# Streamed weights of a hybrid decoder layer, copied once to DRAM piece by piece

## Chip, core, metric

One core of a Trainium2 chip runs one launch of the kernel. The metric is the device time of the launch in microseconds, the median over the runs shown.

## What is computed

One layer of a hybrid decoder, for 1024 prompt tokens, 16 meta tokens and 64 sample tokens (8 sequences of 8), model width 1024, all in float32. The steps, cut to what matters:

```python
hn = rmsnorm(x, norm_mix_w);  proj = hn @ w_in              # u, z, xbc, dt
g = gelu(s5(u));  y_s5 = rmsnorm(g * sigmoid(g @ w_glu))     # w_glu 1024 x 1024
y_m2 = mamba2(z, xbc, dt)                                    # conv, scan by chunks of 128, gate, norm
x = x + concat([y_s5, y_m2]) @ w_out                         # w_out 2048 x 1024
h = rmsnorm(x, norm_ffn_w)
q = h @ w_q                                                  # w_q 1024 x 2048: 8 heads x 2 halves
idx, gate = top16_of_sums(q @ sub_keys)                      # product keys, 128 experts per token
y = rmsnorm(x + sum_k gate_k * gelu(u_tab[idx_k] . h) * v_tab[idx_k])
```

## The kernel before

The program runs in stages, with a barrier of all engines between them: projection (`project_tokens`), S5 scan (`s5_scan`), Mamba (`mamba_scan`), and a last stage, `route_and_experts`, that does mixing, routing and experts. Tokens are handled in 9 tiles of 128 rows: 8 of the prompt and one of the samples and meta tokens. Weights and constants are laid out on the host (`lay_out`): `w_glu`, `w_out` and `w_q` lie in DRAM as 128 partitions x 8 (or 16) row blocks x columns.

**Mamba.** The second half of `mamba_scan` goes over the 8 prompt tiles. On the queue of the sync engine (SP) `load(i)` brings the tile's window for the convolution (`m2s_window`, L1119) and its time steps (`m2s_dt_raw`, L1120), and `store(i)` writes the tile's result `y` to `scratch_ym` (L1124). SP issues `load(0)`, then for each i waits for `window_free`, issues `load(i + 1)` and `store(i)`. VectorE handles tile k in this order: tokens and their product with dt, the first three taps of the convolution of tile k + 1 (`first_taps`, which waits for both transfers of `load(k)`), the decays of tile k, the last tap of tile k + 1, the state and the output of tile k. There is one window buffer. TensorE, ScalarE and GpSimd work on the same tile between VectorE's steps.

**The last stage.** Its tiles are mixed and routed in blocks of 1, 2, 3 and 3 tiles (`BLOCK_OF`). The first block, the opening, runs alone. Then a loop goes over all 1088 row sets of the experts (`NT`): for each, GpSimd gathers 128 expert rows of 8 KB into one of 7 ring buffers (L1521), VectorE takes a dot product (L1812), ScalarE makes the weights (L1621, L1623), and TensorE adds the weighted rows to an accumulator (L1831), after which the ring buffer is free. The steps of block 1 are written into the program between the row sets of tile 0, those of block 2 between the row sets of block 1, those of block 3 between those of block 2; each engine runs its list in order. The last weight load is issued at 3547 us; after the steps of block 3 only row sets remain.

Every block streams all of `w_glu`, `w_out` and `w_q` again, as 20 pieces of 1 MB (128 partitions x 8 row blocks x 256 columns): 4 for `pe_glu` (L1854), 8 for `pe_o` (L1879), 8 for `pe_q` (L1893). Two buffers, `w_buf[:, W % 2]`, take turns: SP's step `sp_w` (`weights`, L1444 to L1461) waits until TensorE is done with the piece two before, then issues the load, and TensorE waits for `w_in` ahead of the piece's first matmul. In SBUF a piece is 8 KB in a row for each partition; in DRAM it is 8 separate runs of 256 floats, 1 KB each:

```python
rows = D["w_q"][:, :, (s - QUERY) * COLS:(s - QUERY + 1) * COLS]
sp.dma_start(w_buf[:, W % WB], rows).then_inc(w_in[W % WB], 16)
```

Of the kernel before, what the change touches and what calls it, by code (L numbers as in the profile page):

```python
# [5 lines left out]
F32 = mybir.dt.float32  # L6
# [6 lines left out]
P = 128  # L13
D_MODEL = 1024
KT = D_MODEL // P
# [36 lines left out]
PH = 8  # L52
# [3 lines left out]
EXPERTS = NK * NK  # L56

LAG = Q + 1
TWO_PI = 2.0 * np.pi
PI_HI = 6.28125  # L60
PI_LO = float(np.float32(TWO_PI - PI_HI))
ROUND = 1.5 * 2.0 ** 23
# [25 lines left out]
def s5_tables(nc, ctx):  # L88

    sb = lambda n, s: ctx.enter_context(nc.sbuf_tensor("s5_" + n, s, F32))  # L90
    return {"power": sb("power", [P, 2, PAIRS, LAG]),
            "down": sb("down", [P, 2, PAIRS, Q]),
# [18 lines left out]
def project_tokens(nc, D, tables):  # L111


    with ExitStack() as ctx:
# [67 lines left out]
        def _(pool):  # L182
# [7 lines left out]

            chain.link(nc.gpsimd.tensor_scalar(T(8), T(2), 1.0 / TWO_PI, ROUND, ALU.mult, ALU.add))
            chain.link(nc.gpsimd.tensor_scalar(T(8), T(8), ROUND, None, ALU.subtract))
# [27 lines left out]

            for n in range(2, LAG):
                complex_mult(power[:, 0, :, n], power[:, 1, :, n], power[:, 0, :, n - 1],
# [168 lines left out]
def s5_scan(nc, D, tables):  # L391
# [4 lines left out]
    with ExitStack() as ctx:  # L396
# [3 lines left out]
        ident = sb("ident", [P, P])  # L400
        out_w = sb("out_w", [P, PAIRS, 2, LAG * S5_CH])
        in_w = sb("in_w", [P, PAIRS, 2, Q * S5_CH])
# [5 lines left out]
        with ExitStack() as c2:  # L408
            sb2 = cur(c2)
            c_in = sb2("c_in", [P, 2, PAIRS, S5_CH])  # L410
            skip = sb2("skip", [S5_CH, S5_GROUPS])
            prod = sb2("prod", [P, PAIRS // 2, LAG, S5_CH])
            prod2 = sb2("prod2", [P, PAIRS // 2, LAG, S5_CH])
            skip_eye = sb2("skip_eye", [S5_CH, S5_GROUPS, S5_CH])
# [48 lines left out]
            def _(dve):  # L463
# [18 lines left out]
                def output_weights(pairs):  # L482

                    shape = [P, PAIRS // 2, LAG, S5_CH]
                    lagged = lambda h: power[:, h, pairs].unsqueeze(3).to_broadcast(shape)
# [308 lines left out]
                        last.then_inc(r_made, 1)  # L794


def mamba_scan(nc, D):


# [2 lines left out]
    with ExitStack() as ctx:  # L802
        sb = lambda n, s, d=F32: ctx.enter_context(nc.sbuf_tensor("m2s_" + n, s, d))
        sem = ctx.enter_context(stage_semaphores(nc, "m2_"))
# [305 lines left out]

        with ExitStack() as c2:
            conv_tail = c2.enter_context(nc.sbuf_tensor("m2m_conv_tail", [P, XB, TAPS - 1], F32))
            prompt_out, tail_ready, window_free = sem("prompt_out"), sem("tail_ready"), sem("window_free")
            block = c2.enter_context(nc.Block())

            @block.sync
            def _(sp):
                def load(i):
                    sp.dma_start(window[:], D["xbc"][:, :, bass.ds(i * P + N_META - TAPS + 1, P + TAPS - 1)]).then_inc(tile_in, 16)  # L1119
                    sp.dma_start(dt_raw[:], D["dt"][bass.ds(i * P, P), :]).then_inc(tile_in, 16)  # L1120

                def store(i):
                    sp.wait_ge(y_ready, i + 3)
                    sp.dma_start(D["ym"][bass.ds(i * P, P), :], y[:].rearrange("p h d -> p (h d)")).then_inc(y_out, 16)  # L1124

                load(0)
                with sp.Fori(0, MAIN_TILES - 1) as i:
                    sp.wait_ge(window_free, i + 1)
                    load(i + 1)
                    store(i)  # L1130
                store(MAIN_TILES - 1)
                sp.wait_ge(state_ready, MAIN_TILES + 2)
                sp.dma_start(D["ssm_end_prompt"], state[:]).then_inc(prompt_out, 16)
                sp.wait_ge(tail_ready, 1)
                sp.dma_start(D["conv_end_prompt"], conv_tail[:]).then_inc(prompt_out, 16)
                sp.wait_ge(prompt_out, 32)
                sp.wait_ge(y_out, 16 * (MAIN_TILES + 2))
# [110 lines left out]
def route_and_experts(nc, D):  # L1248
# [10 lines left out]
    RING = 7  # L1259
    WB = 2  # L1260
    GROUPS, PER = 4, 32
    COLS = D_MODEL // GROUPS
    BLOCK_OF = ((0,), (1, 2), (3, 4, 5), (6, 7, 8))
    NB = max(len(tiles) for tiles in BLOCK_OF)
    FIRST = [tiles[0] for tiles in BLOCK_OF]
# [1 line left out]
    NT = MAIN_TILES * SLOTS + SAMPLE  # L1267
    NG = NT // PER
    UNITS, UNIT = 4, 4
    PIECES = 4 + 8 + PH  # L1270
    GLU, OUT, QUERY = 0, 4, 12

    def block_steps(nb):

# [48 lines left out]
    for b, tiles in enumerate(BLOCK_OF):  # L1323
# [4 lines left out]
        s, room = FIRST[b - 1] * SLOTS, len(BLOCK_OF[b - 1]) * SLOTS - 26  # L1328
# [16 lines left out]
    with ExitStack() as ctx:  # L1345
        sb = lambda n, s, d=F32: ctx.enter_context(nc.sbuf_tensor("pe_" + n, s, d))
        sem = ctx.enter_context(stage_semaphores(nc, "pe_"))
# [6 lines left out]
        ffn_w = sb("ffn_w", [P, D_MODEL])  # L1354
        final_w = sb("final_w", [P, COLS])
        norm_w = sb("norm_w", [P, 2 * KT])
# [3 lines left out]
        w_buf = sb("w_buf", [P, WB, KT, COLS])  # L1360
# [48 lines left out]
        w_in = [sem(f"w_in{n}") for n in range(WB)]  # L1409
# [25 lines left out]
        @block.sync  # L1435
        def _(sp):
            for t, n in ((ident, "ident"), (ones, "ones"), (fold_ident, "fold_ident"), (norm_w, "mix_norm_w"), (ffn_w, "norm_ffn_w"),
                         (count16, "count16"), (keys_t, "keys_t")):
                sp.dma_start(t[:], D[n]).then_inc(consts_in, 16)
            for j in range(GROUPS):  # L1440
                rows, cols = slice(j * PER, j * PER + PER), slice(j * COLS, j * COLS + COLS)
                sp.dma_start(final_w[rows, :], D["final_norm_w"][rows, cols]).then_inc(consts_in, 16)

            def weights(b, s):  # L1444
                W = PIECES * b + s
                if W >= WB:
                    b0, s0 = divmod(W - WB, PIECES)
                    if s0 < OUT:
                        sp.wait_ge(glu_made, KT * b0 + 2 * s0 + 2)
                    elif s0 < QUERY:  # L1450
                        sp.wait_ge(out_made, outs(b0, (s0 - OUT) // 2, s0 % 2, size(b0) - 1))
                    else:
                        sp.wait_ge(q_made, PAIR * b0 + 2 * (s0 - QUERY) + 2)
                if s < OUT:
                    rows = D["w_glu"][:, :, s * COLS:(s + 1) * COLS]
                elif s < QUERY:
                    q, half = divmod(s - OUT, 2)
                    rows = D["w_out"][:, KT - KT * half:2 * KT - KT * half, q * COLS:(q + 1) * COLS]
                else:
                    rows = D["w_q"][:, :, (s - QUERY) * COLS:(s - QUERY + 1) * COLS]  # L1460
                sp.dma_start(w_buf[:, W % WB], rows).then_inc(w_in[W % WB], 16)  # L1461

            def step(name, args):
                if name == "sp_w":
                    weights(*args)
                if name == "sp_y":
                    b, i = args
                    k = FIRST[b] + i
                    if k:
                        pb, pi = HOME[k - 1], k - 1 - FIRST[HOME[k - 1]]  # L1470
                        sp.wait_ge(turned, TURN["pe_m", (pb, pi)] + 1)
                        sp.wait_ge(h_root, FIRST[b])
                        if i == 0:
                            sp.wait_ge(turned, TURN["pe_h", (pb, pi)] + 1)
                    for t, n in ((y5, "y5"), (z, "z"), (ym, "ym")):
                        sp.dma_start(t[:], D[n][k * P:k * P + P, :]).then_inc(y_in, 16)
                if name == "sp_x0":
                    b, i = args
                    k = FIRST[b] + i
                    if b:  # L1480
                        sp.wait_ge(x_mid_out, 16 * FIRST[b])
                        sp.wait_ge(h_ready, FIRST[b])
                    sp.dma_start(x_mid[:, i, :], D["x_all"][k * P:k * P + P, :]).then_inc(x_in, 16)
                if name == "sp_xm":
                    b, i = args
                    k = FIRST[b] + i
                    sp.wait_ge(out_taken, kept(b, 3, i))
                    sp.dma_start(D["x_mid"][k * P:k * P + P, :], x_mid[:, i, :]).then_inc(x_mid_out, 16)
                if name == "sp_x":
                    k = args[0]  # L1490
                    sp.wait_ge(x_mid_out, 16 * (FIRST[HOME[k]] + size(HOME[k])))
                    if k:
                        sp.wait_ge(seeded, GROUPS * k)
                    sp.dma_start(x_now[:], D["x_mid"][k * P:k * P + P, :]).then_inc(x_now_in, 16)
                if name == "sp_st":
                    G = args[0]
                    sp.wait_ge(y_ready, G + 1)
                    for j in range(GROUPS):
                        sp.dma_start(D["y"][G * PER:G * PER + PER, j * COLS:(j + 1) * COLS],
                                     out[j * PER:(j + 1) * PER, G % 2, :]).then_inc(y_out[G % 2], 16)  # L1500

            for name, args in opening:
                step(name, args)
            for n in range(NT):
                for name, args in after[n]:
                    step(name, args)
            for r in range(2):
                sp.wait_ge(y_out[r], 64 * (NG // 2))
# [528 lines left out]
```

## Time and profile before

| | |
|---|---|
| median of 3 runs | 4697.36 us (4696.14 to 4698.72) |
| the profiled execution's own time | 4696.99 us |
| its span, first to last instruction | 4695.2 us |
| TensorE / VectorE / ScalarE / GpSimd busy | 2874.7 / 2492.3 / 1336.4 / 1389.4 us |
| moved by DMA | 1333.53 MB, mean 284 GB/s |
| Mamba's prompt tiles | about 1042 to 1354 us |
| opening (block 0, no gathers) | about 1354 to 1529 us |
| first gather issued | 1529.22 us |

Views are read as follows. A busy time is the sum of an engine's instructions; register, semaphore and DMA-issuing instructions are not counted. The DMA share is the mean busy share of the core's 16 DMA engines; it can come out a little above 1. The DMA queue q0 carries the gathers that GpSimd issues, q1 everything that SP issues.

### The profile page before, as it was taken

The numbers are of one execution on the slowest core, as the hardware profiler recorded it, in microseconds if no ns is written. First come the engines' busy times: TensorE is split into PE (matmuls) and PEld (weight loads), VectorE is DVE, ScalarE is ACT, GpSimd is POOL, SyncE is SP. The second block draws the span as 40 slices with busy tenths as digits, with TensorE's granted clock in tenths as the row PEclk, the third lists the DMA queues.
The fourth block names the chain that finished last, engine by engine and source line by source line (L and its number), as shares of the span: only waits on it lengthen the run. The fifth ranks groups of instructions, "written<-read, shape, count | busy, mean of one in ns | idle before, by whom it ended". The sixth has DMA issues, their size and how long they took to land.

```text
span 4695.2 us, 49395 instructions
## 1 busy us (share of the span) xinstructions
PE 2874.7 (61%) x17200; PEld 1544.7 (33%) x17200; DVE 2492.3 (53%) x5167; ACT 1336.4 (28%) x3229; POOL 1389.4 (30%) x1530
## 2 busy tenths in 40 slices
PE   8999590745555587348876544786666544444444
PEld 5767460723344364114532111353222111111110
DVE  1000529248845339744369955544677864454454
ACT  1110120112221533244333325523333333332322
POOL 3000320301100223333343344333444443333333
PEclk9999755866768798559987655897777555555555
DMA  4111300121135799999999899999999999999999
GB/s 163 55 46 36 75 2 2 43 99 30 46 109 163 287 345 346 348 374 354 365 415 386 339 416 418 409 390 395 414 395 382 403 420 419 420 420 420 420 419 372
DMA packets 337161, 1333.53 MB, mean 284 GB/s; under 512 B 65168, under 2 KB 181776, under 8 KB 197136
## 3 DMA queue, kind: packets, MB, share of 16 engines
q0 software_dynamic: 156672, 1140.92, 59.8%
q1 hardware_dynamic: 180288, 190.03, 12.4%
q8 instruction: 113, 1.85, 0.2%
q14 instruction: 88, 0.72, 0.0%
HBM read 1288.61 MB, written 40.09 MB: 283 GB/s over the span
## 4 chain that ended last, share of the span: by engine, by line
DMA 31%; PE 15%; DVE 15%; ACT 5%; issue 5%; POOL 1%; SPq 0%; DVEq 0%; POOLq 0%; ACTq 0%
DMA pe_ring<-in_uv,pe_index 27%; DVE pe_ring L1812 6%; PE pe_bg L1879 4%; PE pe_acc L1831 4%; DMA pe_w_buf<-in_w_out 3%; PE pe_bg L1854 3%; PE pe_bg L1893 3%; DVE pe_cand L1631 2%; ACT pe_weight L1623 1%; ACT pe_mark L1621 1%; DVE pe_picked L1715 1%; ACT L1621 1%; PE pe_ps_t L1921 1%; DVE pe_best_i L1658 1%; DMA pe_ym<-scratch_ym 1%
## 5 line engine op out<-in xcount | busy, mean ns | idle before, releaser
L1812 DVE CUSTOM_DVE_ANT_0 pe_ring<-pe_ring,pe_h_rep 128x1024 f32<-128x1024 f32 x1088 | 1322.8, 1225 | 1001.3 <-DMA pe_ring<-in_uv,pe_index 978.9
L1521 POOL DMA_INDIRECT pe_ring<-in_uv,pe_index x1088 | 1183.0, 1087 | 2165.6 <-PE pe_acc L1831 1799.7
L1831 PE MATMUL pe_acc<-pe_ring,pe_weight 128*32 128x256 f32 x8704 | 963.7, 537 | 1264.8 <-ACT pe_weight L1623 1241.1
L1831 PEld LDWEIGHTS pe_acc<-pe_ring,pe_weight 128*32 128x32 f32 x8704 | 212.1, 128 | 1955.6 <-ACT pe_weight L1623 1822.4
L1621 ACT ACTIVATE pe_mark<-pe_eye,pe_dot 128x32 f32<-128x32 f32 x1088 | 348.2, 320 | 1629.3 <-DVE pe_dot L1812 1592.6
L1623 ACT ACTIVATE pe_weight<-pe_mark,pe_choice 128x32 f32<-128x32 f32 x1088 | 349.7, 321 | 35.1
L1893 PE MATMUL pe_bg<-pe_in_t,pe_w_buf 128*128 128x384 f32 (+2 forms) x1024 | 322.7, 477 | 9.9 <-DMA pe_w_buf<-in_w_q 8.8
L372 PE MATMUL pj_bank<-pj_w_in,pj_normed_t 128*128 128x512 f32 (+1 forms) x720 | 268.3, 530 | 5.1 <-DMA pj_w_in<-in_w_in 5.1
L1893 PEld LDWEIGHTS pe_bg<-pe_in_t,pe_w_buf 128*128 128x128 f32 x1024 | 205.9, 227 | 130.1 <-issue 67.4
L378 PE MATMUL pj_bank<-pj_normed_t,pj_w_in 128*128 128x128 f32 x1728 | 195.2, 275 | 0.0
L378 PEld LDWEIGHTS pj_bank<-pj_normed_t,pj_w_in 128*128 128x128 f32 x1728 | 193.7, 192 | 0.0
L372 PEld LDWEIGHTS pj_bank<-pj_w_in,pj_normed_t 128*128 128x128 f32 x720 | 126.7, 192 | 141.3 <-issue 141.3
L1879 PE MATMUL pe_bg<-pe_w_buf,pe_m_t 128*128 128x256 f32 x576 | 143.0, 404 | 19.2 <-DMA pe_w_buf<-in_w_out 19.2
L1879 PE MATMUL pe_bg<-pe_w_buf,pe_s_t 128*128 128x256 f32 x576 | 136.8, 392 | 17.2 <-DMA pe_w_buf<-in_w_out 16.1
L1854 PE MATMUL pe_bg<-pe_in_t,pe_w_buf 128*128 128x384 f32 (+2 forms) x512 | 138.6, 427 | 1.6 <-DMA pe_w_buf<-in_w_glu 1.5
L1879 PEld LDWEIGHTS pe_bg<-pe_w_buf,pe_m_t 128*128 128x128 f32 x576 | 113.3, 202 | 50.1 <-DMA pe_w_buf<-in_w_out 22.0
L954 PE MATMUL m2p_a<-m2s_x_dt,m2s_decay 128*128 128x64 f32 x288 | 63.4, 421 | 106.8 <-DVE m2s_decay L850 106.8
L440 POOL MEMSET s5s_b_apart<- 128x512 f32 x1 | 0.5, 524 | 426.2 <-POOLq L108 426.2
L1879 PEld LDWEIGHTS pe_bg<-pe_w_buf,pe_s_t 128*128 128x128 f32 x576 | 109.2, 194 | 45.2 <-DMA pe_w_buf<-in_w_out 18.3
L1621 ACT ACT_TABLE_LOAD x95 | 121.9, 1283 | 5.1 <-DVE pe_dot L1812 3.5
L314 DVE COPY pj_chan_out<-pj_bank 128x512 f32<-128x512 f32 x18 | 12.4, 692 | 192.0 <-PE pj_bank L378 192.0
L1854 PEld LDWEIGHTS pe_bg<-pe_in_t,pe_w_buf 128*128 128x128 f32 x512 | 93.2, 203 | 43.3 <-issue 6.8
(303 smaller groups left out, 3364.7 us busy)
## 6 DMA issues: line engine op xcount, KB each, us to landing
pe_w_buf<-in_w_out SPq DMA_DIRECT2D x32, 1024.0 KB
pe_w_buf<-in_w_q SPq DMA_DIRECT2D x32, 1024.0 KB
pe_ring<-in_uv,pe_index POOLq DMA_INDIRECT x1088
pe_w_buf<-in_w_glu SPq DMA_DIRECT2D x16, 1024.0 KB
m2s_window<-scratch_xbc SPq DMA_DIRECT2D x8, 786.0 KB
pj_w_in<-in_w_in SPq DMA_DIRECT2D x1, 6144.0 KB, 38.8
scratch_xbc<-pj_chan_out SPq DMA_DIRECT2D x8, 768.0 KB, 5.2
pj_x<-in_x_all SPq DMA_DIRECT2D x9, 512.0 KB
```

Of the source, the lines that this page charges most:

```text
L372: last = nc.tensor.matmul(b[:, 0:w], x_t[:, k, :], w_in[:, k, a:a + w], start=k == 0, stop=k == KT - 1)
L378: last = nc.tensor.matmul(b[:, c * P:(c + 1) * P], w_in[:, k, a:a + P], x_t[:, k, :], start=k == 0, stop=k == KT - 1)
L954: last = nc.tensor.matmul(ps_a[:, h // HPG, (h % HPG) * HD:(h % HPG + 1) * HD], decay[:, h, :], x_dt[:, h, :], start=True, stop=True)
L1521: nc.gpsimd.indirect_dma_start(out=ring[:, n % RING, :], out_offset=None, in_=D["uv"], in_offset=bass.IndirectOffsetOnAxis(ap=row, axis=0) ...
L1621: A(mark[:, p, :], eye[:], ACT.Gelu_apprx_tanh, scale=dot[:, p:p + 1]).then_inc(mark_ready, 1)
L1623: A(weight[:, p, :], mark[:, p, :], ACT.Copy, scale=choice[:, k % 2, 1, s:s + 1]).then_inc(weight_ready, 1)
L1631: tt = lambda o, a, b, op: V.tensor_tensor(out=o, in0=a, in1=b, op=op)
L1812: V.tensor_tensor_reduce(out=ring[:, p, 0:D_MODEL], in0=ring[:, p, 0:D_MODEL], in1=h_rep[:, G % 2, :], scale=1.0, scalar=0.0, op0=ALU.mult ...
L1831: last = T.matmul(acc[j * PER:(j + 1) * PER, G % 2, 0:COLS], lhs(j), src[:, j * COLS:(j + 1) * COLS], start=first, stop=final)
L1854: last = T.matmul(bg[:, c % 2, 0:width(b)], w_buf[:, W % WB, kk, c % 2 * P:(c % 2 + 1) * P], wide(in_t_all, b)[:, kk, :], start=kk == 0, s ...
L1879: last = T.matmul(bg[:, (q * size(b) + i) % 4, 0:COLS], src[:, kk, i * P:(i + 1) * P], w_buf[:, W % WB, kk, :], start=half == 0 and kk == ...
L1893: last = T.matmul(bg[:, j % 2, 0:width(b)], w_buf[:, W % WB, kk, j % 2 * P:(j % 2 + 1) * P], wide(in_t_all, b)[:, kk, :], start=kk == 0, s ...
```

## The change

A new DRAM tensor `packed` of 20 pieces, each 128 x 8 x 256 floats in one contiguous block of 1 MB, is written at the start of Mamba's prompt tiles. SP issues the 20 copies, DRAM to DRAM, right after `load(0)`, each with the same source as the weight load that it stands for. At the end of that stage SP waits until all are written. In the last stage `weights` loads `D["packed"][s]` in place of the slice of the weight tensor, for all four blocks, so that a partition's share of a piece is one run of 8 KB. The constants for the pieces move to the top of the file. Nothing else differs.

```diff
+def weight_piece(D, s):
+    if s < OUT:
+        return D["w_glu"][:, :, s * COLS:(s + 1) * COLS]
+    if s < QUERY:
+        q, half = divmod(s - OUT, 2)
+        return D["w_out"][:, KT - KT * half:2 * KT - KT * half, q * COLS:(q + 1) * COLS]
+    return D["w_q"][:, :, (s - QUERY) * COLS:(s - QUERY + 1) * COLS]
...
+            D["packed"] = nc.dram_tensor("scratch_packed", (PIECES, P, KT, COLS), F32).ap()
+            packed_out = sem("packed_out")
...
                 load(0)
+                for s in range(PIECES):
+                    sp.dma_start(D["packed"][s], weight_piece(D, s)).then_inc(packed_out, 16)
                 with sp.Fori(0, MAIN_TILES - 1) as i:
                     sp.wait_ge(window_free, i + 1)
                     load(i + 1)
                     store(i)
                 store(MAIN_TILES - 1)
+                sp.wait_ge(packed_out, 16 * PIECES)
...
-                if s < OUT:
-                    rows = D["w_glu"][:, :, s * COLS:(s + 1) * COLS]
-                elif s < QUERY:
-                    q, half = divmod(s - OUT, 2)
-                    rows = D["w_out"][:, KT - KT * half:2 * KT - KT * half, q * COLS:(q + 1) * COLS]
-                else:
-                    rows = D["w_q"][:, :, (s - QUERY) * COLS:(s - QUERY + 1) * COLS]
-                sp.dma_start(w_buf[:, W % WB], rows).then_inc(w_in[W % WB], 16)
+                sp.dma_start(w_buf[:, W % WB], D["packed"][s]).then_inc(w_in[W % WB], 16)
```

## Rows read from the trace of the kernel before

**Rows 1.** The page's 40 slices of the span: GB/s moved by DMA.

```profile
GB/s 163 55 46 36 75 2 2 43 99 30 46 109 163 287 345 346 348 374 354 365 415 386 339 416 418 409 390 395 414 395 382 403 420 419 420 420 420 420 419 372
```

**Rows 2.** The page's DMA queues (packets, MB, share of 16 engines) and issues.

```profile
q1 hardware_dynamic: 180288, 190.03, 12.4%
...
pe_w_buf<-in_w_out SPq DMA_DIRECT2D x32, 1024.0 KB
...
pe_ring<-in_uv,pe_index POOLq DMA_INDIRECT x1088
```

**Rows 3.** Windows: busy us (count) of PE, PEld, DVE, ACT, POOL; clock, DMA share, GB/s.

```profile
1072.00:1354.00 282.00, 149.13 (x521) 99.90 (x519) 217.90 (x191) 61.03 (x78) 38.55 (x14) 0.69 0.11 34
...
1585.00:1760.00 175.00, 144.14 (x832) 101.13 (x832) 63.95 (x115) 70.02 (x141) 42.57 (x41) 0.94 0.88 315
1760.00:2060.00 300.00, 156.93 (x1028) 75.67 (x1026) 225.66 (x658) 99.80 (x248) 101.21 (x90) 0.67 0.93 362
2105.00:2330.00 225.00, 190.90 (x1104) 118.22 (x1100) 97.43 (x169) 92.81 (x198) 75.81 (x66) 0.93 0.93 351
2330.00:2500.00 170.00, 119.37 (x714) 55.74 (x715) 114.95 (x297) 62.16 (x157) 64.98 (x59) 0.79 1.02 416
...
2905.00:3050.00 145.00, 99.69 (x594) 43.60 (x594) 76.56 (x127) 80.01 (x160) 55.93 (x52) 0.79 1.02 410
3050.00:3205.00 155.00, 124.04 (x794) 88.44 (x794) 69.14 (x121) 39.45 (x112) 51.71 (x46) 0.89 0.98 381
3205.00:3560.00 355.00, 224.27 (x1386) 95.67 (x1378) 232.10 (x587) 123.88 (x323) 149.56 (x132) 0.71 1.01 408
4000.00:4500.00 500.00, 238.96 (x1676) 53.17 (x1676) 251.31 (x413) 152.29 (x432) 191.70 (x198) 0.53 1.01 420
```

**Rows 4.** Chain of waits in order of time: start us, us, what.

```profile
1389.71 5.99 DMA pe_w_buf<-in_w_glu
...
2272.91 16.85 DMA pe_w_buf<-in_w_out
...
3104.65 25.43 DMA pe_w_buf<-in_w_out
```

**Rows 5.** TensorE's waits: opening, blocks 1, 2, 3; us in total, times, longest.

```profile
PE pe_bg L1879 <- DMA pe_w_buf<-in_w_out: 5.2, 5, 2.3
...
PE pe_bg L1893 <- DMA pe_w_buf<-in_w_q: 8.3, 2, 5.8
...
PE pe_bg L1879 <- DMA pe_w_buf<-in_w_out: 3.6, 2, 3.2
...
PE pe_bg L1879 <- DMA pe_w_buf<-in_w_out: 26.6, 3, 11.5
```

**Rows 6.** DMA queues of 1385:1460, 2330:2500, 3050:3205, 4000:4500; packets, MB, share.

```profile
q1 hardware_dynamic: 14651, 15.16, 63.3%
...
q1 hardware_dynamic: 4861, 5.59, 9.4%
...
q1 hardware_dynamic: 7616, 8.00, 14.9%
...
q0 software_dynamic: 28514, 207.68, 100.1%
```

**Rows 7.** Timeline of SP and VectorE, Mamba: start, us, instruction, idle time before.

```profile
1042.73 0.55 SPq L1119 DMA_DIRECT2D m2s_window<-scratch_xbc  x1
1063.53 0.58 SPq L1119 DMA_DIRECT2D m2s_window<-scratch_xbc  x1
...
1048.16 1.76 DVE L850 TENSOR_TENSOR m2s_conv<-m2s_window,m2s_conv_w 128x1536 f32<-128x1536 f32 x1 [16.29 <-DMA m2s_dt_raw<-scratch_dt]
1071.76 1.76 DVE L850 TENSOR_TENSOR m2s_conv<-m2s_window,m2s_conv_w 128x1536 f32<-128x1536 f32 x1 [0.23 <-DVE m2s_x_dt L850]
```

**Rows 8.** DMA issues (median us to landing); the weight line (ns min/median/max).

```profile
scratch_y<-in_x_all SPq DMA_DIRECT2D x1, 192.0 KB, 2.8
...
L1461 SPq DMA_DIRECT2D pe_w_buf<-in_w_q x32: 539/545/550, 1431.7 to 3547.3; - x32
```

More of the change, by code:

```diff
@@ L58 @@
 LAG = Q + 1
+COLS = 256
+PIECES, GLU, OUT, QUERY = 20, 0, 4, 12
 TWO_PI = 2.0 * np.pi
@@ L1261, in route_and_experts @@
     GROUPS, PER = 4, 32
-    COLS = D_MODEL // GROUPS
+    assert COLS == D_MODEL // GROUPS and PIECES == 4 + 8 + PH
     BLOCK_OF = ((0,), (1, 2), (3, 4, 5), (6, 7, 8))
@@ L1269, in route_and_experts @@
     UNITS, UNIT = 4, 4
-    PIECES = 4 + 8 + PH
-    GLU, OUT, QUERY = 0, 4, 12
     def block_steps(nb):
```

## Prediction

> **What bounds the kernel now.** The page's slices came first, for the shape [rows 1]: in the first two fifths of the span the 16 DMA engines are nearly idle, from the middle on they move 340 to 420 GB/s. There the expert rows arrive (1088 gathers of 128 rows of 8 KB), and beside them the streamed weights in 1-KB runs, 80 pieces of 1 MB: 32 of w_out as shown [rows 2], 32 of w_q and 16 of w_glu alike. The stage windows [rows 3] then say what limits each stretch; I read TensorE's and VectorE's busy time against the length and the DMA share. 4000 to 4500 has no weights: DMA 1.01, 420 GB/s, everything else half idle. 1585 to 1760 and 2105 to 2330 are TensorE's (144.1 of 175, 190.9 of 225). 1760 to 2060 is VectorE's (225.7 of 300). 2330 to 2500 and 2905 to 3560 are DMA's (0.98 to 1.02), though 3050 to 3205 reaches only 381 GB/s. The opening, up to 1530, has no gathers yet: a serial chain of weight loads and matmuls. The Mamba stage, 1072 to 1354, is VectorE's: 217.9 of 282.
>
> Third came the chain of waits and TensorE's wait list, for what the weights cost today. Nine weight loads stand among the chain's long pieces, of which one for each stretch is shown [rows 4]: four of up to 6 us in the opening, two of up to 17 in block 2, three of some 25 in block 3. The loads are long because the two DMA queues share the engines: a piece is 64 runs per engine, and 25.43 us / 64 = 0.40 us per run, about one 8-KB gather run (8192 B at 420/16 GB/s is 0.31 us) plus one 1-KB run (2.89 us per MB, below, is 0.047 us). So the engines appear to alternate run by run. But much of each load is covered by other matmuls: TensorE stood still for weights only 5.2 us in the opening, 8.3 in block 1, 3.6 in block 2 and 26.6 in block 3 (the largest entry of each) [rows 5].
>
> **What a run costs.** From the DMA views [rows 6], share times window over MB: weights in 1-KB runs alone (1385 to 1460) 0.633 x 75 / 15.16 = 3.13 us per MB of all 16 engines; beside gathers (3050 to 3205) 0.149 x 155 / 8.00 = 2.89; gathers in 8-KB runs (4000 to 4500) 1.001 x 500 / 207.68 = 2.41. A piece is 1.049 MB: 3.28 or 3.03 us now, 2.53 us in 8-KB runs, a saving of 0.75 us where nothing else runs and 0.50 us beside gathers.
>
> **Added: the copies.** Twenty pieces, 20.97 MB, each read in 1-KB runs. They are issued right behind load(0), and load(1) stands behind all of them in SP's program. All of SP's transfers are one queue, q1 [rows 2]. load(0) is issued at 1042.73 and VectorE starts on it at 1048.16, 5.4 us later; load(1) is issued at 1063.53 and its first use is at 1071.76, with 0.23 us of idle time, so it is in time today [rows 7]. SP issues a 1-MB transfer in about 0.5 us [rows 8], 11 us for twenty, so the engines and not SP set the pace. If the queue is served in order, the copies stream from about 1047.5, and at the uncontended 3.13 us per MB take 65.7 us, to 1113.2. load(1) then needs at most its 5.4 us: 1118.6, and 4 us if its start-up hides under the copies. First use goes from 1071.8 to about 1118: **46 us lost**. Nothing covers it: the first taps of tile 2 stand ahead of the decays and the output of tile 1 in VectorE's order, so VectorE idles, and TensorE, ScalarE, GpSimd and SP's store(0) behind it. The later loads come 35 us apart with the copies gone, and the stage's end moves by the whole amount. The new wait for the copies at the stage's end costs nothing: they are done 230 us earlier.
>
> Bounds of this: no transfer of this size from DRAM to DRAM is in the trace. The nearest row is a 192-KB one, landed in 2.8 us [rows 8], no worse than the stores around it. Below: 2.89 us per MB gives 60.6 us and a loss of 41; if the copies kept the 8-KB pace of 2.41, 50.5 us and 31. Above: if reads and writes together can't pass the 420 GB/s that is the most any row shows, 41.9 MB take 100 us and the loss is 80. I take 46, as read runs of this shape were measured at that pace.
>
> **Changed: 80 loads in 8-KB runs.** By stretch:
> - Opening: four loads are on the chain [rows 4], 0.75 us each: 3.0 us. Bounds 0 and the 5.2 us that TensorE waits.
> - Block 1: 8.3 us of waits on two w_q pieces, in the stretch that is VectorE's; a piece beside gathers will land in 8 x (0.31 + 0.31) = 5 us, so the waits go, but VectorE's work remains. I take 5, between 0 and 8.3. No DMA saving is counted while its share is 0.88 to 0.93.
> - Block 2: the 3.6 us wait stands in TensorE's stretch and goes whole. In 2330 to 2500, 5.59 MB fall from 0.094 x 170 = 16.0 to 13.5 us, 2.5 us. Together 6; bounds 2.5 and 3.6 + 20 x 0.50 = 13.6.
> - Block 3, 3050 to 3205: three waits of together 26.6 us, during which the ring of seven rows fills and gathers stop. TensorE's busy time is 124.0, so without the waits DMA is next: the 381 GB/s x 155 us = 59.1 MB at 420 GB/s are 140.6 us instead of 155, **14.4 us**. This holds both the freed stalls and the shorter runs. Bounds 8 (a wait half removed) and 26.6.
> - Block 3, the other 12 pieces, with DMA at 1.01: 12 x 0.50 = 6; I take 5, as 3400 to 3560 is partly VectorE's; bounds 3 and 10.
>
> Sum of gains 3 + 5 + 6 + 14.4 + 5 = 33.4 us; bounds 13.5 and 63.7. The issue on SP stays one instruction per piece. Net: 46 - 33.4 = +12.6 us. The profiled execution took 4696.99 us by its own time, 1.8 more than its span, and the median is 4697.36; on the median, 4710 us.
>
> **A rule against the change.** Shorter runs are dearer here: 2.89 to 3.13 against 2.41 us per MB [rows 6]. The Trainium skill, page "DMA: Bandwidth & Descriptors", section "Specifications", puts the least transfer for line rate at 512 B; by that a 1-KB run would already be at full rate, and the rows of this case differ. As a mechanism it is the third rival below.
>
> **The rivals.**
> 1. *The weights were worth more (faster).* All of TensorE's waits for weights become time (5.2 + 8.3 + 3.6 + 26.6 = 43.7) and block 2 and 3's forty pieces save 0.50 us each (20): 63.7 us; with the copy at its lower 41 us the time is 4675. For it: the 25-us loads on the chain. Against: DMA at 0.98 to 1.02 leaves no room for more than 14 us in 3050 to 3205. It decides once the gain passes 55 us. Chance 0.12.
> 2. *The copies are bound by DRAM, reading and writing at once.* 100 us, loss 80, net +47: 4744. For it: no row shows such a stream. Against: the 2.8-us row. Chance 0.15. The Trainium skill, page "HBM Reference", section "Specifications (TRN2)", gives 716 GB/s for the memory of two cores, an estimate of 58.6 us for 41.9 MB by itself, no bound here; no run here shows it.
> 3. *The run's length buys nothing in rate.* The gains lose opening 3, block 2's 2.5, block 3's 5 and 8.00 MB x 0.48 = 3.8 us: 19 remain, net +27: 4724. Against it stand [rows 6]. Chance 0.05.
> 4. *load(1) isn't held behind the copies*, or they hide: loss under 15 us, net -20: 4677. For it: the DMA engines are at 0.11 in that stage. Against: one queue, one order of issue. Chance 0.08.
> 5. *The loads still come in 1-KB runs.* Only the 46 us remain: 4743. Against: the copy is laid out as the buffer is. Chance 0.03.
>
> **Numbers.** The forecast case, a stall of 41 to 52 us against gains of 28 to 42, holds 0.57 and runs from -1 to +24, that is 4696 to 4721. A measurement of this kernel tells a change from none at about 0.2%, 9.4 us. Of the 0.57, 0.35 lies above +9.4 and 0.22 within it. Slower: 0.35 + 0.15 + 0.05 + 0.03 = 0.58. Faster: 0.12 + 0.08, less 0.05 for weak forms that stay within 9.4 us: 0.15. Same: 0.22 + 0.05 = 0.27. The range goes to 4685 below, leaving out the stronger half of rivals 1 and 4, and to 4742 above, leaving out the worse half of rival 2.
>
> **What would show it.** Right: VectorE idle some 46 us before its first convolution of tile 2, released by tile 2's loads; SP issuing 20 copies in 1044 to about 1100; q1 packets down from 180288 by 81920 - 10240 - 20480, if a copy counts 1-KB runs; TensorE's waits for weights under 10 us in all; 3050 to 3205's work, moved, at 410 GB/s or more; no weight load over 10 us on the chain. Wrong: a stall under 30 or over 60 us; waits for weights that stay; or these waits gone and the gathers' stretch no shorter, which would mean that DMA was the bound there all along.

## The result

The changed kernel takes 4718.41 us, median of 6 runs (4716.02 to 4722.68), against 4697.81 us for the kernel before (6 runs): a ratio of 1.0043, 95% interval 1.003 to 1.0056. It is slower by about 20 us. The prediction said 4710 us and slower, with a range of 4685 to 4742.

The loss comes in one place. In the timeline of SP and of VectorE (start us, us, instruction, idle time before it and what ended it), the kernel after shows, as the counterpart of [rows 7] (the first three copies one by one, the others merged by tensor):

```profile
1045.05 0.60 SPq L1142 DMA_DIRECT2D scratch_packed<-in_w_glu  x1
1045.69 1.55 SPq L1142 DMA_DIRECT2D scratch_packed<-in_w_glu  x1
1047.28 2.73 SPq L1142 DMA_DIRECT2D scratch_packed<-in_w_glu  x1
...
1052.73 27.21 SPq L1142 DMA_DIRECT2D scratch_packed<-in_w_out  x8
1079.98 29.27 SPq L1142 DMA_DIRECT2D scratch_packed<-in_w_q  x8
1109.62 3.15 SPq L1133 DMA_DIRECT2D m2s_window<-scratch_xbc  x1
...
1121.02 1.76 DVE L862 TENSOR_TENSOR m2s_conv<-m2s_window,m2s_conv_w 128x1536 f32<-128x1536 f32 x1 [48.66 <-DMA m2s_dt_raw<-scratch_dt]
```

Before, load(1) was issued at 1063.53 and VectorE used it with 0.23 us of idle time. Now SP gets to it at 1109.62, since it is held at the copies: the first goes out in 0.60 us, the second in 1.55, the third in 2.73, and the last sixteen take about 3.5 us each, which is the pace at which the engines move them (below). VectorE then idles 48.66 us. The DMA queue of 1048 to 1113 (packets, MB, share of 16 engines) gives the pace:

```profile
DMA packets 20038, 20.10 MB, mean 309 GB/s; under 512 B 400, under 2 KB 20038, under 8 KB 20038
...
q1 hardware_dynamic: 20038, 20.10, 101.7%
```

1.017 x 65 / 20.10 = 3.29 us per MB, 69.0 us for the 20.97 MB, or 3.45 us for one copy. The last stage's first transfer goes from 1354.00 to 1400.67: 46.7 us lost by the end of the Mamba stage, of which 1.0 us was there before its load(0) (1042.73 to 1043.71).

The gain comes in the last stage. TensorE's waits for weights (line, cause: us in total, times, longest), from 1340 to 1600 and from 1600 to 2020, as the counterpart of [rows 5]; from 2020 on there is none left where 30.2 us stood before:

```profile
PE pe_bg L1887 <- DMA pe_w_buf<-scratch_packed: 4.2, 3, 1.8
PE pe_bg L1862 <- DMA pe_w_buf<-scratch_packed: 0.6, 1, 0.6
...
PE pe_bg L1887 <- DMA pe_w_buf<-scratch_packed: 0.8, 1, 0.8
```

The weight loads among the chain's long pieces (start us, us), as the counterpart of [rows 4]; the longest was 26 us, now it is 9:

```profile
1431.82 4.82 DMA pe_w_buf<-scratch_packed
1454.69 4.73 DMA pe_w_buf<-scratch_packed
1463.22 5.51 DMA pe_w_buf<-scratch_packed
1472.52 4.73 DMA pe_w_buf<-scratch_packed
1706.15 9.20 DMA pe_w_buf<-scratch_packed
```

And the stretch of block 3 that took 155 us at 381 GB/s in [rows 3], as a window of the kernel after and with its DMA queues:

```profile
3082.00:3224.00 142.00, 124.37 (x798) 85.82 (x802) 69.83 (x121) 38.70 (x109) 55.71 (x49) 0.95 1.01 420
...
q0 software_dynamic: 7068, 51.47, 87.4%
q1 hardware_dynamic: 1344, 8.00, 13.6%
```

The same TensorE work, 124 us, now fits in 142 us, with DMA at 1.01 and 420 GB/s. The 8.00 MB of weights cost 0.136 x 142 / 8.00 = 2.41 us per MB, what the gathers cost, in place of 2.89 in [rows 6].

To see where the gain falls I counted the gathers in GpSimd's timeline (0 to 1087) and took the start of the same gather in both traces:

| gather | what begins | before | after | later by |
|---|---|---|---|---|
| 0 | tile 0's row sets, block 1's steps | 1529.22 | 1573.59 | 44.4 |
| 128 | block 2's steps | 1999.77 | 2044.54 | 44.8 |
| 384 | block 3's steps | 2795.07 | 2832.48 | 37.4 |
| 480 | | 3062.17 | 3097.15 | 35.0 |
| 512 | | 3167.73 | 3190.90 | 23.2 |
| 768 | no more steps | 3866.50 | 3884.89 | 18.4 |
| 1087 | last | 4671.64 | 4690.68 | 19.0 |

So the opening returns 2.3 us (46.7 to 44.4), block 1 nothing, block 2 some 7, block 3 19.0, of which 11.8 between gathers 480 and 512. These are two single executions. In the experiments below, blocks whose loads were left as they were moved by up to 7 us, and block 2 is the one that moved most, so its 7 us can't be put down to the loads alone. The last table of the experiments takes all traces together.

### The profile page after: what moved, and what is told of

Its sections match the earlier page's. It is cut to its first block, busy times and chain, and to the rows that moved or that the text cites. A ratio compares the mean times of both kernels' runs of the same rounds, so it can differ in the third digit from the quotient of the medians.

```text
span 4714.2 us, 49416 instructions
## 1 busy us (share of the span) xinstructions
PE 2870.3 (61%) x17200; PEld 1540.2 (33%) x17200; DVE 2491.4 (53%) x5167; ACT 1336.9 (28%) x3229; POOL 1387.9 (29%) x1530
## 3 DMA queue, kind: packets, MB, share of 16 engines
q1 hardware_dynamic: 129408, 211.01, 13.0%
## 4 chain that ended last, share of the span: by engine, by line
DMA 30%; PE 15%; DVE 15%; ACT 5%; issue 4%; POOL 1%; SPq 0%; DVEq 0%; POOLq 0%; ACTq 0%
DMA pe_ring<-in_uv,pe_index 29%; DVE pe_ring L1820 6%; PE pe_acc L1839 4%; PE pe_bg L1887 4%; PE pe_bg L1901 3%; PE pe_bg L1862 2%; DVE pe_cand L1639 2%; ACT pe_weight L1631 1%; ACT pe_mark L1629 1%; DMA pe_ym<-scratch_ym 1%; DVE pe_picked L1723 1%; ACT L1629 1%; PE pe_ps_t L1929 1%; DVE pe_best_i L1666 1%; DVE pe_rest L1667 1%
## 5 line engine op out<-in xcount | busy, mean ns | idle before, releaser
L1901 PEld LDWEIGHTS pe_bg<-pe_in_t,pe_w_buf 128*128 128x128 f32 x1024 | 203.5, 224 | 119.6 <-issue 66.1
L862 POOL TENSOR_TENSOR m2s_da_upto<-m2s_da,m2s_upto 128x2048 f32<-128x2048 f32 x8 | 28.9, 3609 | 298.5 <-DVE m2s_da L862 298.5
L966 PEld LDWEIGHTS m2p_a<-m2s_x_dt,m2s_decay 128*128 128x128 f32 x288 | 61.6, 329 | 160.2 <-DVE m2s_decay L862 160.2
```

Source lines behind the costliest of these rows:

```text
L966: last = nc.tensor.matmul(ps_a[:, h // HPG, (h % HPG) * HD:(h % HPG + 1) * HD], decay[:, h, :], x_dt[:, h, :], start=True, stop=True)
L1901: last = T.matmul(bg[:, j % 2, 0:width(b)], w_buf[:, W % WB, kk, j % 2 * P:(j % 2 + 1) * P], wide(in_t_all, b)[:, kk, :], start=kk == 0, s ...
```

## The experiments

Each is compared with executions of the kernel before on the same chip; the edits shown are against the changed kernel. Theory A is the prediction's: the loss is load(1)'s place in one queue behind the copies, the gain is the 8-KB runs.

**Copies dealt out.** Instead of 20 copies behind load(0):

```diff
+                def copies(first, last):
+                    for s in range(first, last):
+                        sp.dma_start(D["packed"][s], weight_piece(D, s)).then_inc(packed_out, 16)
                 load(0)
-                for s in range(PIECES):
-                    sp.dma_start(D["packed"][s], weight_piece(D, s)).then_inc(packed_out, 16)
-                with sp.Fori(0, MAIN_TILES - 1) as i:
+                copies(0, 2)
+                for i in range(MAIN_TILES - 1):
                     sp.wait_ge(window_free, i + 1)
                     load(i + 1)
+                    copies(2 + 3 * i, min(5 + 3 * i, PIECES))
                     store(i)
```

> The 20 copies are dealt out: 2 behind load(0), 3 behind each of the next loads, so that each tile's loads stand ahead of them. Theory A (the 46.7 us were lost because load(1) stood in one queue behind all copies, and the 28 us were won by the 8-KB loads): the wait of 48.7 us goes, the gain stays: 4670 us, 4666 to 4676. Theory B (the copies cost the Mamba stage by what they take of the DMA engines and of DRAM, wherever they are issued): at least half of the loss stays: 4690 us or more.

Measured: 4671.86 us (5 runs) against 4699.27, ratio 0.9942, interval 0.9929 to 0.9956, 27 us faster than before. Every byte is still copied in the same stage, but VectorE's waits for loads, in the wait list of 1040 to 1360, are what they were (the kernel before, then this one: us in total, times, longest):

```profile
DVE m2s_conv L850 <- DMA m2s_dt_raw<-scratch_dt: 31.2, 7, 16.3
DVE m2s_conv L862 <- DMA m2s_dt_raw<-scratch_dt: 30.0, 7, 16.1
```

The longest stands ahead of tile 1 in both. Theory A holds; theory B falls. This version beats both kernels.

**Copies alone.** The change's copies, with the old loads:

```diff
-                sp.dma_start(w_buf[:, W % WB], D["packed"][s]).then_inc(w_in[W % WB], 16)
+                sp.dma_start(w_buf[:, W % WB], weight_piece(D, s)).then_inc(w_in[W % WB], 16)
```

> The change's copies where the change has them, but the last stage loads its weights in 1-KB runs from the original tensors. Theory A: only the loss is left: 46.7 us above before, 4744 us, 4741 to 4749, with the wait of some 48.7 us ahead of tile 2's first taps. Theory B agrees about the sum. If some of the gain were due to something else than the loads from the copy, the time would lie under 4740 us.

Measured: 4749.15 us (4 runs), ratio 1.0106 (1.009 to 1.0121), 50 us slower (42 to 57), at the upper end of what was expected. VectorE's idle time ahead of tile 2's first taps in this trace:

```profile
1118.16 1.76 DVE L862 TENSOR_TENSOR m2s_conv<-m2s_window,m2s_conv_w 128x1536 f32<-128x1536 f32 x1 [46.58 <-DMA m2s_dt_raw<-scratch_dt]
```

Without the loads from the copy no gain is left. The 3 us beyond the stall lie within the interval.

**Copies behind load(1).** SP waits for `window_free`, issues load(1), then all 20 copies, then goes on as before:

```diff
                 load(0)
+                sp.wait_ge(window_free, 1)
+                load(1)
                 for s in range(PIECES):
                     sp.dma_start(D["packed"][s], weight_piece(D, s)).then_inc(packed_out, 16)
-                with sp.Fori(0, MAIN_TILES - 1) as i:
+                store(0)
+                with sp.Fori(1, MAIN_TILES - 1) as i:
```

> All 20 copies in one go, but behind load(1) in place of load(0). load(2) is needed 36.1 us after load(1), the copies start 20.0 us later. Theory A (the stall is the end of the copies less the time at which the next load is needed): the wait moves to tile 3's first taps and is 48.7 - 16.1 = 32.6 us: 4702 us, 4698 to 4707. Theory B (a cost of the copies wherever they stand): 4718 us.

Measured: 4702.94 us (10 runs), ratio 1.0009 (1.0 to 1.0018). The wait moved to tile 3 and is 33.38 us, 32.6 were worked out:

```profile
1139.67 1.76 DVE L862 TENSOR_TENSOR m2s_conv<-m2s_window,m2s_conv_w 128x1536 f32<-128x1536 f32 x1 [33.38 <-DMA m2s_dt_raw<-scratch_dt]
```

So the stall is set by when the copies end, and the load behind them lands, against when that load is needed.

**The copy read in 1-KB runs.** As dealt out, with each piece laid out row block by row block (`RUN` is 1):

```diff
-            D["packed"] = nc.dram_tensor("scratch_packed", (PIECES, P, KT, COLS), F32).ap()
+            D["packed"] = nc.dram_tensor("scratch_packed", (PIECES, KT // RUN, P, RUN, COLS), F32).ap()
...
-                sp.dma_start(w_buf[:, W % WB], D["packed"][s]).then_inc(w_in[W % WB], 16)
+                sp.dma_start(w_buf[:, W % WB].rearrange("p (a k) c -> p a k c", k=RUN),
+                             D["packed"][s].rearrange("a p k c -> p a k c")).then_inc(w_in[W % WB], 16)
```

> As spread, but each piece of the copy is laid out row block by row block, so that the load from the same contiguous 1 MB still comes in 1-KB runs, 64 for each DMA engine. Theory A (the run's length wins the 28 us): no gain is left: 4697 us, 4692 to 4703, and TensorE's waits for weights are back at 30 us or more. Rival C (reading one contiguous block of DRAM wins them, not the run's length): as spread, 4670 us.

Measured: 4697.83 us (11 runs), ratio 0.9999 (0.999 to 1.0008). The wait list from 2900 on and the window of block 3's stretch show the old picture, 30 us of waits and 373 GB/s:

```profile
PE pe_bg L1892 <- DMA pe_w_buf<-scratch_packed: 30.1, 3, 11.8
...
3047.00:3203.00 156.00, 122.68 (x783) 88.00 (x785) 67.61 (x119) 38.58 (x110) 51.67 (x45) 0.89 0.96 373
```

Rival C falls: it is the run's length. It also shows once more that the dealt-out copies, and the loop of SP that is written out for them, cost nothing that can be measured.

**2-KB runs.** The same with RUN = 2; each piece's copy is issued as two of 512 KB.

> As spread, but a piece comes in 2-KB runs, 32 for each DMA engine. Beside gathers a piece should land in 32 x (0.31 + 0.09) = 13 us, in time for TensorE, and cost the engines about half of what 8-KB runs save. Theory A (the gain has two parts: about 12 us from TensorE's waits for late pieces, about 15 us from cheaper engine time): waits under 10 us, and 12 + 7 = 19 us of gain: 4680 us, 4676 to 4684. Rival E (only the late pieces matter): as spread, 4672 us. Rival F (only the engine time matters): half the gain, 4686 us.

Measured: 4675.96 us (5 runs), ratio 0.996 (0.9946 to 0.9974), 19 us faster by the ratio, 12 to 25, and 22 between the medians. Window and queue of block 3's stretch:

```profile
3050.00:3195.00 145.00, 120.22 (x785) 80.54 (x784) 68.17 (x120) 42.32 (x114) 59.19 (x50) 0.93 1.02 415
...
q1 hardware_dynamic: 4558, 9.05, 16.4%
```

0.164 x 145 / 9.05 = 2.63 us per MB, about half way from 2.89 to 2.41, and no wait for weights is left from 2900 on. The median lies at the lower end of theory A's 4676 to 4684. The interval holds theory A's 19 us and also F's 13.5, and ends just below E's 27, which is itself known only as 21 to 33; so the division into late pieces and cheaper runs is not settled.

**Which blocks.** Three kernels, the copies dealt out, with the old load in some blocks:

```diff
-                sp.dma_start(w_buf[:, W % WB], D["packed"][s]).then_inc(w_in[W % WB], 16)
+                sp.dma_start(w_buf[:, W % WB], D["packed"][s] if b == 3 else weight_piece(D, s)).then_inc(w_in[W % WB], 16)
```

Block 1 alone on the old loads (`b != 1`):

> As spread, but block 1 alone loads its 20 pieces in 1-KB runs from the original tensors. Theory A (in block 1 VectorE and TensorE set the pace, and its 8.3 us of waits for weights were no loss): as spread, 4672 us, 4668 to 4676, although the waits on two pieces of w_q come back. If the waits had been worth what the prediction took, 5 us: 4677 us.

Only block 3 on the copy (`b == 3`):

> As spread, but only block 3 loads from the copy, the opening and blocks 1 and 2 from the original tensors. Theory A: block 3 holds 19 of the 28 us, since there DMA sets the pace and the long waits stand: 4680 us, 4676 to 4684. If the gain were alike in all blocks (7 us for each 20 pieces): 4692 us.

Only the opening and blocks 1 and 2 on the copy (`b != 3`):

> The counterpart of only_block3: the copies dealt out as in spread, the opening and blocks 1 and 2 load from the copy, block 3 from the original tensors. The prediction's terms for these three were 3 + 5 + 6 = 14 us: 4684 us, 4681 to 4687. Theory A as the runs so far read (the opening's 2 to 3 us are real, block 1's waits are worth nothing, of block 2's at most the 3.6 us): 4 to 6 us of gain: 4693 us, 4689 to 4697.

| on the copy | median us (runs) | before us | ratio, interval | gain us |
|---|---|---|---|---|
| all | 4671.86 (5) | 4699.27 | 0.9942, 0.9929 to 0.9956 | 27 |
| all but block 1 | 4672.82 (5) | 4698.03 | 0.9948, 0.9934 to 0.9962 | 24 |
| block 3 | 4674.91 (5) | 4698.03 | 0.9954, 0.994 to 0.9968 | 22 |
| opening, blocks 1, 2 | 4692.41 (11) | 4698.72 | 0.9986, 0.9977 to 0.9995 | 6.6 |

(The gain is 1 less the ratio, times 4698.) The last two add up to the first within their intervals. The kernel with only block 3 on the copy came out just under its 4676 to 4684: 22 us by the ratio, where one trace had given 19. In the kernel without block 1 the old wait is there again, in the list from 1600 to 2020:

```profile
PE pe_bg L1905 <- DMA pe_w_buf<-in_w_q: 6.1, 1, 6.1
```

The time is as good with it to within the intervals, which are too wide to rule out the 5 us of the prediction.

The traces taken together tell more. For each stretch of the last stage, the change of its length against the trace of the kernel before, in us, as mean (lowest to highest), with the old 1-KB runs and with 8-KB runs there; the kernel with 2-KB runs is left out, the kernel before counts as 0:

| stretch | 1-KB runs (traces) | 8-KB runs (traces) | gain us |
|---|---|---|---|
| opening, first transfer to gather 0 | 1.4 (0.0 to 4.0) (4) | -0.9 (-2.3 to 0.8) (5) | 2.2 |
| block 1's steps, gathers 0 to 128 | 2.1 (-0.6 to 4.8) (5) | 1.4 (-1.7 to 4.1) (4) | 0.7 |
| block 2's steps, 128 to 384 | -3.5 (-6.7 to 0.0) (4) | -7.0 (-9.5 to -4.2) (5) | 3.6 |
| block 3's steps, 384 to 768 | 2.5 (0.0 to 5.8) (4) | -19.4 (-20.3 to -18.1) (5) | 21.9 |

Only in block 3 do the two columns lie apart. It holds about three quarters of the gain; what block 2 gives is about half of the 7 us that the first comparison showed. With 2-KB runs block 3's stretch is 15.2 us shorter, or 17.7 of the 21.9 us; that is one execution, and it settles the division between late pieces and cheaper runs no more than the medians do.

## Why the prediction was right

**The copies: right, a little small.** The wait stands where it was put, ahead of tile 2's first taps, and is 48.66 us where 46 were taken. The pace more than accounts for it: 3.29 us per MB where 3.13 were taken from the opening's loads, which is 3.4 us over 20.97 MB. The same copies left 46.58 us in the kernel with the copies alone, so two executions differ by as much as the miss. Where load(1) was held differs from the prediction's sum, by which SP issues all twenty in 11 us: SP was itself held, as the prediction's signs had it ("1044 to about 1100"), so load(1) stood in SP's program until 1109.62 and only then in the DMA queue. The order of issue, which made the loss, is the same. The lower bound (8-KB pace) and rival 2, DRAM as the limit, are out. That the stage's end would move by nearly the whole stall was right too (46.7 us). Rival 4, copies that hide, needs only another place for them, as the dealt-out copies show: the DMA engines had the room, the queue's order took it. Copies issued by another engine than SP were not tried.

**Block 3: right.** 14.4 us were forecast for 3050 to 3205 with DMA as the next bound, 5 for the other pieces. The window is 142 us, 13 shorter, at DMA 1.01; the block as a whole 19.0 us shorter in the trace, 22 us (15 to 28) in the kernel with only block 3 on the copy. How much of it is the waits and how much the cheaper runs is open.

**Opening: right.** 3.0 forecast, 2.3 in the trace, 2.2 over all traces.

**Blocks 1 and 2: mis-sized.** The terms "I take 5" (block 1) and "Together 6" (block 2) are the ones that came out too large; over all traces they are 0.7 and 3.6. With the opening they made 14 us; the kernel with block 3 on the old loads gains 6.6, interval 2.3 to 10.8. For block 1, the trace moved by 0.4 us although its 8.3 us of waits went down to 0.8, and the kernel that keeps its old loads is no slower that can be measured. For block 2, the 3.6 us of waits that were to go whole were one execution's: three other traces with 1-KB runs there show 0.6 (copies alone), 0.2 (the copy read in 1-KB runs) and 0.9 (only block 3 on the copy). That VectorE's work in block 1 takes up what TensorE no longer waits for is argued from its 225.7 us of 300 in [rows 3]; no run shows it directly.

**The sum.** Gains of 33.4 were forecast; 28 are in the trace (46.7 less the 19.0 of the last gather), 27 in the kernel with the copies dealt out. So +12.6 became +20: 2.7 us from the stall, the rest from blocks 1 and 2. Both misses push the same way, so nothing cancelled. Rival 1's 55 us of gain was far off. Rivals 3 and 5 are out: q1 shows 129408 packets where 180288 - 81920 + 10240 + 20480 = 129088 were worked out, and 2.41 us per MB. Smaller readings are off without bearing on the sum: the DMA engines are nearly idle for the first third of the span rather than two fifths (287 to 346 GB/s in the fourteenth to sixteenth slice, [rows 1]); and 0.40 us per run is a tenth above the 0.36 of one gather run and one 1-KB run, and equal groups of runs taken in turn would give that sum as well, so that the engines alternate run by run is not shown.

**The rule.** By the Trainium skill, page "DMA: Bandwidth & Descriptors", section "Specifications", line rate starts at 512 B. The runs here do not agree: 2.89 us per MB in 1-KB runs, 2.63 in 2-KB runs, 2.41 in 8-KB runs, all beside the same gathers.

## What to carry to other kernels

A bulk transfer that has time to spare still takes a place in its queue: put it behind the load that is needed next, in portions that end before the one after it is issued. Here that is the whole difference between 20 us lost and 27 us won. When a stream of short runs shares the DMA engines with long ones, estimate its landing time as runs times (its own run plus the other stream's run), and look at which engine waits for it. Here that gave 23 us for 64 1-KB runs, where the chain shows 25 to 26, and 5 us for a piece in 8-KB runs, where one took 9.20, so it is a lower estimate. And lengthening the runs is worth most where that wait empties the stream that sets the pace, and little where another engine is the bound.

## What was not expected of the hardware

A stream from DRAM to DRAM in 1-KB runs kept up 309 GB/s (320 in the kernel with the copies alone), which is as much read as written at once, 618 GB/s together: the totals of the profile's page rise by 20.97 MB read and 20.97 MB written. The prediction had allowed that 420 might be the limit of the sum. And SP ran ahead of the engines by about two such transfers only: from the third copy on each took 2.5 to 6.1 us to issue, and after the last was issued 2.75 MB were still moved (1109.62 to 1121), of which 0.8 are load(1).
